# The shared expert's second layer moved into the loop, and two small inputs brought by transfers instead of products

## The reference

```python
x = x + W_out[ mLSTM heads | pooling heads ](rmsnorm(x) @ W_in)
scores = sigmoid(xn @ router_w)            # then top 8 of 64, in the best 4 of 8 groups
hb = silu(xn @ ex_w1) * (xn @ ex_w3)       # of each row's 8 experts
routed = sum over them of (hb * gate) @ ex_w2
shared = (silu(xn @ sh_w1) * (xn @ sh_w3)) @ sh_w2
x = x + routed + shared
x = x + (p @ w_ple_proj) * sigmoid(rmsnorm(x) @ w_ple_gate)
```

## Time and profile before

| | us |
|---|---|
| median of three runs | 1046.06 (1044.48 to 1046.35) |
| the profiled execution | 1048.96 |
| its span, first to last instruction | 1047.2 |
| TensorE busy | 990.8 (95%) |
| VectorE busy | 454.8 (43%) |
| GpSimd busy | 358.6 (34%) |
| ScalarE busy | 148.3 (14%) |
| mean granted TensorE clock | 0.986 of full speed |
| bytes moved by DMA | 295.92 MB, 283 GB/s over the span |

### The profile page before, as it was taken

How to read it: one execution, slowest core, us unless ns; L and a number is a source line. 1 busy time by engine, 2 the same in 40 slices (tenths; PEclk the granted TensorE clock), 3 DMA queues, 4 the chain that set the end, 5 groups by cost and what they waited for, 6 DMA issues and landing times.

```text
span 1047.2 us, 16054 instructions
## 1 busy us (share of the span) xinstructions
PE 990.8 (95%) x5696; PEld 454.3 (43%) x5696; DVE 454.8 (43%) x1309; ACT 148.3 (14%) x364; POOL 358.6 (34%) x439
## 2 busy tenths in 40 slices
PE   7999999999999999999999998999899898899996
PEld 5777555555554433333333333333333333333343
DVE  3411222345549654344434443434433433342885
ACT  3100023301021101000011000011000000012322
POOL 6000321211024444444544554344434443440132
PEclk9999999999999999999999998999989999999999
DMA  8132222222159599999999999999999999958932
GB/s 268 29 92 81 81 97 72 75 56 61 41 155 377 208 369 407 406 408 411 403 414 410 415 413 414 387 409 409 409 374 412 412 393 395 399 200 313 421 127 81
DMA packets 77188, 295.92 MB, mean 283 GB/s; under 512 B 17258, under 2 KB 27690, under 8 KB 50261
## 3 DMA queue, kind: packets, MB, share of 16 engines
q1 hardware_dynamic: 60573, 257.62, 63.2%
q0 software_dynamic: 16576, 37.80, 9.4%
HBM read 276.56 MB, written 32.54 MB: 295 GB/s over the span
## 4 chain that ended last, share of the span: by engine, by line
PE 63%; DMA 23%; DVE 5%; issue 4%; POOL 2%; SPq 1%; DVEq 1%; ACT 1%; POOLq 0%; ACTq 0%
PE bank L1908 22%; DMA ring<-in_ex_w 16%; PE bank L2286 10%; PE bank L2263 8%; PE bank L2283 7%; PE bank L2347 5%; DMA arena<-xs_dram,slot 4%; PE bank L2266 2%; PE bank L1914 2%; DMA arena<-y_dram 1%; POOL arena L924 1%; PE bank L2001 1%; DMA x<-in_x_prompt 1%; PE bank L2011 1%; PE bank L2048 1%
## 5 line engine op out<-in xcount | busy, mean ns | idle before, releaser
L924 POOL DMA_INDIRECT arena<-xs_dram,slot x200 | 219.0, 1095 | 70.7 <-issue 63.2
L2283 PE MATMUL bank<-arena 128*32 128x512 f32 x1536 | 226.2, 594 | 0.0
L939 POOL DMA_INDIRECT y_dram<-arena,outrow x48 | 49.1, 1023 | 264.8 <-DVE slot L1710 218.1
L2286 PE MATMUL bank<-ring,arena 128*128 128x512 f32 x256 | 118.8, 619 | 18.4 <-DMA ring<-in_ex_w 17.5
L2283 PEld LDWEIGHTS bank<-arena 128*32 128x32 f32 x1536 | 60.1, 110 | 137.8 <-issue 133.9
L2283 PE MATMUL bank<-xT,arena 128*32 128x512 f32 x256 | 112.9, 594 | 0.0
L2283 PE MATMUL bank<-mixpj,arena 128*32 128x512 f32 x256 | 112.9, 594 | 0.0
L1724 DVE STREAM_TRANSPOSE arena<-arena 128x1024 f32<-128x1024 f32 x50 | 62.2, 1244 | 80.3 <-DMA arena<-xs_dram,slot 74.0
L1908 PE MATMUL bank<-xT,ring 128*128 128x288 f32 x384 | 93.4, 406 | 0.0
L2263 PE MATMUL bank<-arena 128*32 128x512 f32 x512 | 87.1, 595 | 0.8 <-ACT arena L1136 0.8
L2286 PEld LDWEIGHTS bank<-ring,arena 128*128 128x128 f32 x256 | 49.6, 199 | 77.5 <-issue 66.3
(11 more groups left out here) (412 smaller groups left out, 1248.1 us busy)
## 6 DMA issues: line engine op xcount, KB each, us to landing
arena<-in_ex_w SPq DMA_DIRECT2D x88, 1024.0 KB
ring<-in_ex_w SPq DMA_DIRECT2D x64, 1024.0 KB
arena<-y_dram SPq DMA_DIRECT2D x18, 1024.0 KB, 11.1
xT<-in_ex_w SPq DMA_DIRECT2D x16, 1024.0 KB
mixpj<-in_ex_w SPq DMA_DIRECT2D x16, 1024.0 KB
ring<-in_w_in SPq DMA_DIRECT2D x5, 2048.0 KB, 9.4
wide<-in_ex_w SPq DMA_DIRECT2D x8, 1024.0 KB
ring<-in_w_out SPq DMA_DIRECT2D x2, 2048.0 KB, 9.0
```

Source lines behind the costliest of these rows:

```text
L924: pool.indirect_dma_start(xg[b][:, 256 * a:256 * a + 256], None, xs_quarter, bass.IndirectOffsetOnAxis(slot[k][:, a:a + 1], 0), bounds_che ...
L939: pool.indirect_dma_start(y_dram, bass.IndirectOffsetOnAxis(outrow[b][:, 0:1], 0), og[b], None, bounds_check=K * T - 1, oob_is_err=False). ...
L2283: ins = pe.matmul(bank[2][t, :], xgT[b][:, c, t], w13[k if lane < 3 else k4][:, :, wc, :], start=(c == 0), stop=(c == KT - 1))
L2286: ins = pe.matmul(bank[2][:, :], xgT[b][:, c, :], w13[k][:, :, wc, :], start=(c == 0), stop=(c == KT - 1))
```

## The change

- g1 is loaded as 8 rows of 128 (`g1_row`), turned by TensorE and copied by VectorE.
- M's first 512 columns go to DRAM (`m_dram`) and come back spread over the partitions, one transfer for a head, into the two halves of `g_b`'s space (`m_bc`); the four "Mb" products go. `g_b` itself is loaded after the last use of `m_bc`.
- `second` and all its adds leave the stretch before the loop. The turned results are kept in five buffers of their own (`hTs`). sw2 moves to the second half of the shared first-layer weights' space and is loaded once `first(4)` is done, ahead of buffer 3's expert; the p tiles move to the start of mixpj; w_pj, whose space sw2 now has, is loaded at the end of the loop.
- Before the loop TensorE's order becomes turn, five eighths of `first(3)`, "pos", the rest of it, "ord", turn, `first(4)`, the p tiles, then picks and turns. VectorE reads the order out before two copies, and transposes the first gathered rows before it builds the third one-hot. Buffer 4's expert is loaded once the p tiles are drained and the router's scratch is read.
- The loop's second turn (steps 6 to 11) is written out too. TensorE runs `second_late` after each of steps 6 to 10, in banks 0 and 1, and before the second to fifth of them waits for the adds of the one before (`s_lated`). VectorE runs `late_add` after each of steps 7 to 11: it waits for the products, adds them to x and clears the buffer.

The diff, cut:

```diff
-    g = []
+    g = [(("g1",), "v")]
...
-        g += [(("Mb", h), "v")] + [(("S", h, j), "v") for j in range(4)]
+        g += [(("S", h, j), "v") for j in range(4)]
...
-    g += [(("shT", 0), "s"), (("sh", 2), "s")] + halves("y", 0, "v") + [(("pos",), "v")]
-    g += [(("shT", 1), "s"), (("sh", 3), "s"), (("ord",), "v")] + halves("y", 1, "v") + [(("pk", 0), "v")]
-    g += [(("shT", 2), "s"), (("sh", 4), "s")] + halves("y", 2, "v") + [(("pk", 1), "v")]
-    g += [(("shT", 3), "s")] + [(("pT", i), "s") for i in range(NT)] + halves("y", 3, "v")
-    g += [(("pk", 2), "v"), (("shT", 4), "s")] + halves("y", 4, "v")
+    g += [(("shT", 0), "s"), (("sh", 2), "s"), (("shT", 1), "s"), (("pos",), "v"), (("sh", 3), "s"), (("ord",), "v")]
+    g += [(("shT", 2), "s"), (("sh", 4), "s")] + [(("pT", i), "s") for i in range(NT)] + [(("pk", 0), "v")]
+    g += [(("shT", 3), "s"), (("pk", 1), "v"), (("shT", 4), "s"), (("pk", 2), "v")]
...
+        m_dram = nc.dram_tensor("m_dram", [H, SEQ], F32).ap()
...
+        m_bc = [g_b[:, SEQ * b:SEQ * b + SEQ] for b in range(2)]
...
+        g1_row = sb("g1_row", [KT, P])
...
-        sw2 = mixpj[:, 0:2 * DM].rearrange("p (c n) -> p c n", n=DM)
-        ptile = mixpj[:, 2 * DM:2 * DM + NT * PLE].rearrange("p (i n) -> p i n", n=PLE)
-        sel_at = 2 * DM + NT * PLE
+        sw2 = arena[:, sh_at + 2 * DM:sh_at + 4 * DM].rearrange("p (c n) -> p c n", n=DM)
+        ptile = mixpj[:, 0:NT * PLE].rearrange("p (i n) -> p i n", n=PLE)
+        sel_at = NT * PLE
+        shared_at = [KT * T, KT * T + 2 * P, WORDS, WORDS + 2 * P]
+        hTs = [mixpj[:, n:n + 2 * P].rearrange("p (c t) -> p c t", t=P) for n in shared_at]
+        hTs += [xT_flat[:, WORDS:WORDS + 2 * NS].rearrange("p (c t) -> p c t", t=NS)]
...
-            sp.dma_start(g1, norm_mix_g[0].rearrange("(c p) -> p c", p=P),
-                         allow_slow_non_contiguous=True).then_inc(s_ga, 16)
+            sp.dma_start(g1_row[:, :], norm_mix_g[0].rearrange("(c p) -> c p", p=P)).then_inc(s_ga, 16)
...
             load_chunk("k")
-            sp.dma_start(g_b[:, :], bc(norm_ffn_g[0])).then_inc(s_gb, 16)
             sp.dma_start(bufnat, state_pool[0].rearrange("b r c -> (b r) c")).then_inc(s_state, 16)
             sp.dma_start(wp, w_pool[0].rearrange("g c d -> c g d")).then_inc(s_state, 16)
 
...
             load_chunk("v")
+            sp.wait_ge(s_mrow, 1)
+            sp.dma_start(m_dram, M_row[:, 0:SEQ]).then_inc(s_mst, 16)
+            sp.wait_ge(s_mst, 16)
+            for h in range(2):
+                sp.dma_start(m_bc[h], bc(m_dram[h])).then_inc(s_mbc[h], 16)
             load_chunk("o")
             load_chunk("wo0")
...
+            for h in range(2, H):
+                sp.wait_ge(s_dif, NP_ * (h - 1))
+                sp.dma_start(m_bc[h % 2], bc(m_dram[h])).then_inc(s_mbc[h % 2], 16)
             load_chunk("wo1")
+            sp.wait_ge(s_dif, NP_ * H)
+            sp.dma_start(g_b[:, :], bc(norm_ffn_g[0])).then_inc(s_gb, 16)
...
             after(sp, "wo", NP_, 0)
-            sp.dma_start(sw2, sh_w2[0].rearrange("(c p) n -> p c n", p=P)).then_inc(s_sh2, 16)
             wait_drained(sp, "nout")
...
             after(sp, "sh", NT - 1)
+            sp.dma_start(sw2, sh_w2[0].rearrange("(c p) n -> p c n", p=P)).then_inc(s_sh2, 16)
             sp.wait_ge(s_order, 2)
             e = expert(3)
             load13(3, e)
             load2(3, e)
-            for n in range(2):
-                sp.dma_start(w_pj[:, :, n], w_ple_proj[0, :, 512 * n:512 * n + 512].rearrange("(c p) n -> p c n", p=P)
-                             ).then_inc(s_pj, 16)
             e = expert(7)
-            after(sp, "y", NT - 1, 0)
+            sp.wait_ge(s_split, 2)
             wait_drained(sp, "pT", NT - 1)
             load13(4, e)
             load2(4, e)
...
+            sp.wait_ge(s_lated, passes * len(LATE))
+            for n in range(2):
+                sp.dma_start(w_pj[:, :, n], w_ple_proj[0, :, 512 * n:512 * n + 512].rearrange("(c p) n -> p c n", p=P)
+                             ).then_inc(s_pj, 16)
             sp.wait_ge(s_mm1, more * STEPS + (STEPS - 2))
...
-                drain("s", act.copy(hT[:, :, 0:r], b[:, 0:2 * P].rearrange("p (c t) -> p c t", t=P)[:, :, 0:r]),
-                      "shT", i)
+                drain("s", act.copy(hTs[i], b[:, 0:2 * P].rearrange("p (c t) -> p c t", t=P)[:, :, 0:r]), "shT", i)
...
                 b = full_bank(act, "pT", i)
                 if i == 0:
-                    act.wait_ge(s_order, 2)
+                    act.wait_ge(s_order, 3)
                 r = ROWS[i]
                 drain("s", act.copy(pT(i), b[:, 0:2 * P].rearrange("p (c t) -> p c t", t=P)[:, :, 0:r]),
                       "pT", i)
+            sht(3)
             sht(NP_)
...
-            dve.wait_ge(s_ga, 16)
+            b = full_bank(dve, "g1")
+            drain("v", dve.tensor_copy(g1, b[:, 0:KT]), "g1")
+            wait_drained(dve, "g1")
...
-                b = full_bank(dve, "Mb", h)
...
+                dve.wait_ge(s_mbc[h % 2], 16 * (h // 2 + 1))
                 if h:
                     dve.wait_ge(s_pt, NP_ * h)
                     dve.wait_ge(s_msk, NP_ * h)
                 for j in range(NP_):
 
-                    dve.tensor_scalar(D[:, BLK[j]:BLK[j + 1]], b[:, P * j:SEQ], anat[:, 0, j, h:h + 1], 0.0,
+                    dve.tensor_scalar(D[:, BLK[j]:BLK[j + 1]], m_bc[h % 2][:, P * j:SEQ], anat[:, 0, j, h:h + 1], 0.0,
                                       ALU.subtract, ALU.max).then_inc(s_dif, 1)
-                dve.wait_ge(s_dif, NP_ * h + NP_)
-                drain("v", dve.memset(small[0:1, 30:31], 0.0), "Mb", h)
...
             weigh(late)
-            add_x("y", 0)
             dve.wait_ge(s_const, 5)
...
             link(dve.tensor_single_scalar(quo_i, place_i, 5, ALU.arith_shift_right))
+            b = full_bank(dve, "ord")
+            dve.tensor_scalar(order[0:1, 0:NE], b[0:1, 0:NE], 0.25, None, ALU.add).then_inc(s_order, 1)
+            drain("v", dve.tensor_scalar(np_k[:, :], b[0:1, NE:NE + 8], 0.25, None, ALU.add), "ord")
             link(dve.tensor_copy(tquo[:, 0:NE, :].rearrange("p e i -> p i e"), quo_i))
             link(dve.tensor_single_scalar(quo_i, place_i, 31, ALU.bitwise_and))
             link(dve.tensor_copy(tmod[:, 0:NE, :].rearrange("p e i -> p i e"), quo_i))
-            b = full_bank(dve, "ord")
-            dve.tensor_scalar(order[0:1, 0:NE], b[0:1, 0:NE], 0.25, None, ALU.add).then_inc(s_order, 1)
-            drain("v", dve.tensor_scalar(np_k[:, :], b[0:1, NE:NE + 8], 0.25, None, ALU.add), "ord")
+            dve.sem_inc(s_order, 1)
             wait_drained(dve, "ord")
-            dve.wait_ge(s_order, 2)
+            dve.wait_ge(s_order, 3)
             dve.wait_ge(s_split, 2)
...
             one_hot(1, 0, heads[0])
-            add_x("y", 1)
...
-            add_x("y", 2)
+            heads += [expert(4)]
             first_index(1)
+            turned_rows(64, 0)
             one_hot_shared(3, 2, 0, heads[2], heads[3], 1)
-            add_x("y", 3)
-            heads += [expert(4)]
             first_index(2)
             one_hot(4, 1, heads[4])
-            turned_rows(64, 0)
             turned_rows(64, 1)
-            add_x("y", 4)
...
+                def late_add(at, i):
+
+                    dve.wait_ge(s_late, at)
+                    if i == NP_:
+                        dve.tensor_tensor(x[0:NS, i, 0:512], bank[0][0:NS, :], x[0:NS, i, 0:512], ALU.add)
+                        dve.tensor_tensor(x[0:NS, i, 512:DM], bank[0][NS:P, :], x[0:NS, i, 512:DM], ALU.add)
+                    else:
+                        for n in range(2):
+                            c = slice(512 * n, 512 * n + 512)
+                            dve.tensor_tensor(x[:, i, c], bank[n][:, :], x[:, i, c], ALU.add)
+                    dve.memset(hTs[i], 0.0).then_inc(s_lated, 1)
+
                 for j in range(UNROLL):
                     step(r * STEPS, r * (STEPS * 8), r * (STEPS * 32), r * (2 * PERIODS), 0, j, j == 0)
-                with dve.Fori(1, TURNS) as n:
+                for j in range(UNROLL):
+                    step(r * STEPS + UNROLL, r * (STEPS * 8) + UNROLL * 8, r * (STEPS * 32) + UNROLL * 32,
+                         r * (2 * PERIODS) + 4, LOADS, j)
+                    if j:
+                        late_add(r * len(LATE) + j, LATE[j - 1])
+                with dve.Fori(2, TURNS) as n:
                     for j in range(UNROLL):
                         step(r * STEPS + n * UNROLL, r * (STEPS * 8) + n * (UNROLL * 8),
                              r * (STEPS * 32) + n * (UNROLL * 32), r * (2 * PERIODS) + n * 4, n * LOADS, j)
...
+            pe.wait_ge(s_ga, 16)
+            b = free_bank(pe, "g1")
+            pe.transpose(b[:, 0:KT], g1_row[:, :], ident[0:KT, 0:KT]).then_inc(filled, 1)
...
-                b = free_bank(pe, "Mb", h)
-                pe.matmul(b[:, :], sel4[:, h, :], M_row[:, 0:SEQ], start=True, stop=True).then_inc(filled, 1)
```

(71 more changed lines are left out.)

34 lines of the change are left out of this document (22 added, 12 removed).

## The result

| | kernel before | changed kernel |
|---|---|---|
| median, us | 1045.27 (4 runs) | 1082.74 (4 runs) |
| range, us | 1044.37 to 1046.35 | 1079.94 to 1085.27 |
| profiled execution, its span | 1048.96, 1047.2 | 1085.27, 1083.5 |
| mean granted clock | 0.986 | 0.975 |

The change makes the kernel slower: the ratio is 1.0349, 95% interval 1.0327 to 1.037, or 37.5 us between the medians. The forecast had the direction, the place and the pair of engines (late products on TensorE that wait for VectorE's adds), but two such waits where four came, and 10.5 us instead of 37.5. The time lies far above its range (1042.0 to 1063.0).

A forecast was written before the change was run, and what follows sets the result against it. TensorE's products outside the expert loop and the expert weights' loads within it were taken as the bound. Terms -1.6 - 4.1 - 2.0 + 18.3 = +10.6, say +10.5 us, gave 1056.5 us; range 1042 to 1063.

The forecast's parts named there:

- g1 as rows: Kernel's opening: loading g1 as 8 rows lets q's products start earlier, gain 1.6 us, bounds 0 and 2.3.
- The maximum by transfers: Ahead of the loop: four heads each lose one "Mb" product of 1.05 us on TensorE, gain 4.1 us.
- the stretch before the loop: Shared products leave, first gather starts 3.7 us ahead, loop's first product comes 2.0 us earlier, bounds 0.5 and 6.
- The second turn: Steps 6 to 11: five late products and two waits of about 5.3 us make it 24.8 us later, bounds 17.8 and 30.
- Rival C: Second turn: the adds keep up, no new wait, 1042.7 us in all; chance 0.06.
- The clock: Second turn: TensorE at half clock after each of two waits, 1.7 us each, 3.4 in all, within the 24.8.
- Absorbed by the weights: Loop: the weights' stream, 6.5 us behind TensorE (from 4 to 9), absorbs that much of the second turn's 24.8 us.
- what the gain ahead is worth: Ahead of the second turn: the gains of 1.6, 4.1 and 2.0 us count in full at the end, 7.7 us.
- rival B: Loop's end hangs on DMA alone, second turn free up to its lag; 1038.4 us with lag over 25 us; chance 0.17.
- The tail: Kernel's end: p products run beside the read-back of y, other banks may cost 0.3 us; counted as nothing.
- The signs: Expected in the profile: q's products at 19.1 us, output products 5.7 us earlier, idle TensorE and lower DMA share in second turn.
- tiles 1 and 3 only: Second turn: TensorE waits for adds only ahead of the late products of tiles 1 and 3, some 5 us each.

The follow-up runs named there:

- Experiment 8: Kernel before, with one of four experts loading only half of its second-layer weights: 1031.15 us, ratio 0.9852.
- experiment 5: Changed kernel with the adds moved between hh and the bank's emptying, and the first transposed gather back behind the third and fourth one-hot: 1044.41 us, ratio 0.9982.
- experiment 1: Changed kernel, with VectorE's late adds moved up between hh and the emptying of the second-layer bank: 1047.59 us, ratio 1.0000.
- Experiment 3: Changed kernel, with the adds behind VectorE's transposed gather and ahead of its one-hot: 1070.82 us, ratio 1.0216.
- experiment 4: Changed kernel, with the late products and their adds in the loop's fifth turn instead of its second, VectorE's order as changed: 1074.07 us, ratio 1.0265.
- experiment 7: Changed kernel with the adds ahead of the one-hot, the same kernel as Experiment 3 run once more: 1070.87 us.
- experiment 2: Changed kernel without the five shared second-layer products and their adds, part of the result missing: 1046.81 us, ratio 0.9988.
- experiment 6: Kernel of experiment 5, with the five late products in the loop's fifth turn instead of its second: 1042.05 us, ratio 0.9954.

## Why the prediction failed, step by step

The profiled executions differ by 36.3 us in span; the forecast's sum was 10.6. The 26 us between them lie in three places: 4 ahead of the second turn, 19 in it, 3 behind it.

**g1 as rows (-1.6).** Not shown. The start of q's products scatters over 3.5 us between executions of the same code, and the means with and without the change are equal. A term of 1.6 us was read from one execution of a place that repeats no better than that. The prediction also had q's products wait for the queue behind g1; by the chain they wait for the last of x and the norm, and the landing of x scatters by 2.2 us.

**The maximum by transfers (-4.1) and the stretch before the loop (-2.0).** The sum was right, but by luck. From q's start to the loop's first product the changed order takes 336.4 us in the changed kernel (358.86 less 22.43) instead of 342.8: -6.4 where -6.1 was forecast. VectorE's eighth addition of an output product to x lies between the two terms (first the kernel before, then the changed one):

```profile
295.24 0.69 DVE L1456 TENSOR_TENSOR x<-bank,x 128x512 f32<-128x512 f32 x1 [5.99 <-PE bank L1908]
```
```profile
290.54 0.69 DVE L1475 TENSOR_TENSOR x<-bank,x 128x512 f32<-128x512 f32 x1 [5.99 <-PE bank L1940]
```

Up to it, from q's start, are 268.1 us instead of 274.5, and from it to the loop's first product 68.3 in both. Experiment 8, with the code of before, repeats 274.5 and 68.3, and every execution with the changed code repeats 268.1. So the maximum by transfers gave 6.4 us where 4.1 were forecast, and the stretch before the loop gave nothing where 2.0 were. Of the 6.4 us, 4.7 are there when the last head's small products start. The other 1.7 are in the first output product, which the kernel before ran at a granted clock of 0.81 and the changed one at 1.00:

```profile
215.08 8.80 PE L1908 MATMUL bank<-ring,mixpj 128*128 128x512 f32 x16 [0.83 <-issue]
```
```profile
212.07 7.10 PE L1940 MATMUL bank<-ring,mixpj 128*128 128x512 f32 x16 [0.83 <-issue]
```

TensorE's waits just ahead of it are nearly the same in both (1.6, 1.2 and 0.8 us against 1.5, 1.3 and 0.8); what kept the clock up is open. In the stretch before the loop the first gather's issue came 2.2 us nearer to the output products, not 3.7; its rows landed 5.65 us behind the last issue, not 5.2; and the first product came 5.0 us behind the start of their transpose, not 4.5. The third one-hot need not stand behind that landing: with it ahead, the loop's first product starts 3.4 us earlier in experiment 5. Missed was the clock as well: after 12.1 us without work the first layer takes 9.68 us instead of 7.13, with a granted clock of 0.50 (1.2 GHz) in 350 to 360 us. The end of step 6's second layer was 3.5 us ahead in the profiled execution, 5.2 if counted from q's start, where the forecast had 7.7 and 6.1.

**The second turn (+24.8), the waits.** This is the step that failed. Its products were sized nearly right: 73.0 us for the five steps without a wait; experiment 1 took 71.5, because the fifth product, of the sample's 64 tokens, takes 1.95 us and not 3.6. It named the right wait and the right engine, and the adds of tile 0 did end 20 to 22 us after e (at 460.07, 21.2 us after 438.86). But it reached that number by the wrong road, so that its fit is luck. "second_late(2) is not held" and "second_late(4) is not held" rest on the chain from the *previous* step's second layer over the gather. The forecast itself said that the adds stand "behind the whole of step 6+n", and then took from that step only the transposed gather and the one-hot. Ahead of both, in the same step, stands the emptying of bank 6 (a half of the second layer's result), which waits for the second layer of the *same* step. So every late product but the first is held until 6.5 us (with a shared one-hot; 5.3 with a plain one) after its own step's second layer: 0.8 for the bank, 0.6 for the index, 1.25 for the transposed gather, 2.3 or 1.2 for the one-hot with its register loads, 1.5 for the adds. Four waits, 23.7 us, instead of two of 5.3. Experiment 3 took the one-hot out of this sum and the waits fell to 3.8 us, as worked out beforehand; experiment 1 took all of it out and they were gone. Rival C had the right remedy in its last sentence ("if the adds stood elsewhere in VectorE's order"), and I didn't ask whether the adds in their place could ever be in time.

**The clock (+3.4).** Each wait paid, and there were four: the late products took 5.11, 6.37 and 6.58 us instead of 3.44, the last one 3.69 instead of 1.95 and the first layer behind it 8.00 instead of 7.00, together 10.5 us or 2.6 per wait against the 1.7 taken. With the 71.5 us of experiment 1 this is 71.5 + 23.7 + 10.5 = 105.7, which is the row. The prediction left two views open. The Trainium skill's ("TensorE: Matmul & The Clock Gate", "HAM oscillation — how this bites in real kernels": a block of products behind a wait for data starts cold) is borne out by all eight waits of 4.9 to 6.4 us in the changed kernel and experiment 4, at 1.7 to 3.2 us each. Of the eight waits of 3.7 to 3.9 us in experiments 3 and 7, seven paid 1.6 to 3.0 us and one 0.3, so at that length the other view, that some waits cost no clock, stands too.

**Absorbed by the weights (-6.5), and what the gain ahead is worth (-7.7).** The idea was right, its use was not. Against the kernel without late products the second turn was 12.9, 35.7 and 47.1 us longer in experiments 1, 3 and the changed kernel, and cost 1.3, 23.9 and 37.8: 11.6, 11.8 and 9.3 us were absorbed, more than the 6.5 taken. But a stream that absorbs a delay absorbs a gain as well. The sum let the transfers swallow 6.5 us of the second turn and passed the 7.7 us won ahead of it to the end in full, as if there were no stream. The traffic from about 400 us on was saturated, and an earlier TensorE hardly moves it: the 8.7 us that experiment 2 is ahead at step 11 are 1.3 us at the end.

**The lag.** That the absorbed amount would grow with the lag was rival B's idea. In the fifth turn, where the kernel before already waits for weights, experiment 4 absorbed 13.7 us of 42.7 (the turn took 106.7 us, and 64.0 in experiment 2), against 9.3 in the second. So B's 25 us or more were never to be had; the buffers, and not how far the weights are behind, seem to limit it. That limit was not tried by itself.

**The tail.** As forecast, level: 0.5 us.

**The signs.** Ahead of the loop they failed in part: q's products started 1.7 us later instead of 1.6 earlier, the output products came 4.7 us earlier instead of 5.7, and the loop's first product also 4.7, not 2 us more. In the second turn they came: idle TensorE ahead of the late products, the lower clock behind, the DMA share under 1 and the later wait for weights (ahead of a first layer from step 39 on, instead of 21). The sign "tiles 1 and 3 only" was the one that told against the forecast.

## What to carry to other kernels

When work is appended to an engine's step, follow *every* instruction ahead of it in that same step to what it waits for, in the same turn of the loop, and then look for the idle place of that engine where the new work would be in time: here 3.0 us lay free between two instructions, and using them was worth 36 us. Where a stream of transfers is saturated, sum only the time in which it is made to be idle: delays and gains of the engines beside it both vanish into it up to the room in the buffers, and a sum must not take the one in full and the other not. Late work belongs where the transfers alone set the pace, with its producer and consumer placed so that neither waits: the fifth turn instead of the second was worth 2.9 us here (experiment 6 against 5), at the edge of what these runs can tell, and with the waits left in (experiment 4) it was still 29.0 us above no late products.

## What the runs showed of the hardware

- Behind each of the four waits of 4.9 to 6.4 us the granted clock was 0.50 (1.2 GHz). These stretches of the changed kernel begin with the late products of tiles 1 to 4, and TensorE is busy in all of them. After 12.1 us without work the first layer took 2.6 us more. Of eight waits of 3.7 to 3.9 us, one was followed by the full clock (experiment 7, 1.00 and 3.70 us).

```profile
460.10:462.10 2.00, 1.97 (x3) 0.94 (x4) 0.00 (x0) 0.00 (x0) 1.70 (x2) 0.50 0.91 373
481.50:483.50 2.00, 2.00 (x3) 0.97 (x4) 0.00 (x0) 0.00 (x0) 1.49 (x2) 0.50 0.96 317
505.00:507.00 2.00, 2.00 (x3) 0.97 (x4) 0.00 (x0) 0.00 (x0) 1.70 (x2) 0.50 1.01 401
529.00:531.00 2.00, 1.99 (x6) 0.78 (x8) 0.00 (x0) 0.00 (x0) 1.56 (x2) 0.50 0.56 204
```

- The start of a kernel repeats worse than its loop: q's products started anywhere from 18.96 to 22.43 us in nine profiled executions with the same opening, while the 336 us behind them up to the loop repeated within 0.9 us; the last of x that the chain waits for landed anywhere from 10.2 to 12.3 us. A change to the opening needs many executions, or a wait that can be seen to vanish.
- VectorE worked strictly in the order of its instructions: the adds' product had been ready for 16 us (442.7 to 458.6) and was not touched. The Trainium skill states it ("PSUM — Partial Sum Buffer", "Engine vs sequencer instructions": the queues of ScalarE, VectorE and GpSimd are strict FIFO), and these rows agree.
